# Convolution taps that read PSUM, and new step orders, in a twelve-stage fp32 block kernel on one Trainium2 core

## The reference, cut to what matters

```python
def causal_dwconv(x, w, b):            # CONV_W = 4 taps a channel
    y = lax.conv_general_dilated(x, w[:, None, :], window_strides=(1,),
        padding=((CONV_W - 1, 0),), dimension_numbers=("NWC", "WIO", "NWC"),
        feature_group_count=c)
    return y + b

def hybrid_mixer(h, w_in, w_out, ...):
    proj = h @ w_in
    pa, pb, pc = jnp.split(proj, [2 * A_WIDTH, 2 * A_WIDTH + B_IN], axis=-1)
    gate_a, rec_a = jnp.split(pa, 2, axis=-1)
    rec = causal_dwconv(rec_a, lru_conv_w, lru_conv_b)         # 384 channels
    ya = rg_lru(rec, ...) * jax.nn.gelu(gate_a)                # gated scan over time
    yb = ssd_mixer(pb, ...)      # silu(causal_dwconv(xbc)) on 896 channels, chunked state space
    yc = chunk_sgu(pc, ...)      # gelu, layer norm, masked 128 x 128 spatial mix
    return jnp.concatenate([ya, yb, yc], axis=-1) @ w_out
```

## Time and profile before

| | |
|---|---|
| median of 3 runs | 1957.23 us (1957.09 to 1957.32) |
| profiled execution | 1958.12 us |
| its span, first to last instruction | 1956.8 us |
| PE busy | 1926.5 us, 98% |
| DVE, ACT, POOL busy | 1204.0, 1098.7, 168.5 us (62, 56, 9%) |
| mean granted TensorE clock | 0.998 |
| DMA | 350 MB, 179 GB/s over the span |

### The profile page before, as it was taken

How to read it: one execution, slowest core, us unless ns; L and a number is a source line. 1 busy time by engine, 2 the same in 40 slices (tenths; PEclk the granted TensorE clock), 3 DMA queues, 4 the chain that set the end, 5 groups by cost and what they waited for, 6 DMA issues and landing times.

```text
span 1956.8 us, 24460 instructions
## 1 busy us (share of the span) xinstructions
PE 1926.5 (98%) x9304; PEld 1602.6 (82%) x9304; DVE 1204.0 (62%) x1863; ACT 1098.7 (56%) x1903; POOL 168.5 (9%) x219
## 2 busy tenths in 40 slices
PE   7999999999999999999999999999999999999999
PEld 6888888888788798888888888888888888888887
DVE  6555787555755578755665566665566556666554
ACT  5554776554655576655565555655555555565553
POOL 6000131000000013000000004100000000410000
PEclk9999999999999999999999999999999999999999
DMA  7564636554566463565465645355556554435553
GB/s 250 194 222 162 202 106 198 191 186 162 194 228 205 133 212 109 185 201 194 151 213 191 195 156 162 112 190 194 194 172 193 189 195 156 163 112 190 194 193 108
DMA packets 96773, 350.23 MB, mean 179 GB/s; under 512 B 10896, under 2 KB 11024, under 8 KB 96400
## 3 DMA queue, kind: packets, MB, share of 16 engines
q1 hardware_dynamic: 94176, 339.57, 52.2%
q10 hardware_dynamic: 2448, 9.09, 1.6%
q0 software_dynamic: 32, 0.00, 0.0%
HBM read 347.57 MB, written 1.05 MB: 178 GB/s over the span
## 4 chain that ended last, share of the span: by engine, by line
PE 90%; DVE 4%; POOL 2%; issue 1%; ACT 1%; DMA 0%; SPq 0%; ACTq 0%; POOLq 0%; DVEq 0%
PE ps_gu L397 18%; PE ps_gu L399 17%; PE ps_gu L398 17%; PE ps_acc L397 9%; PE ps_acc L399 9%; PE ps_acc L398 9%; PE ps_tr L444 2%; PE ps_gu L630 1%; PE ps_gu L631 1%; PE ps_gu L632 1%; DVE sb_wl L1867 1%; PE ps_acc L417 1%; DVE sb_scratch L2067 1%; DMA sb_x<-x 0%; DVE sb_wl L1862 0%
## 5 line engine op out<-in xcount | busy, mean ns | idle before, releaser
L397 PE MATMUL ps_gu<-sb_wh,sb_xh 128*128 128x512 f32 (+2 forms) x1600 | 642.8, 402 | 6.1 <-DVE sb_xl L1914 4.6
L399 PE MATMUL ps_gu<-sb_wh,sb_xl 128*128 128x512 f32 (+2 forms) x1600 | 624.3, 390 | 0.0
L398 PE MATMUL ps_gu<-sb_wl,sb_xh 128*128 128x512 f32 (+2 forms) x1600 | 621.9, 389 | 0.0
L1862 DVE SCALAR_TENSOR_TENSOR sb_wl<-sb_raw,sb_gpre,sb_wh 128x512 fp32r<-128x512 f32 x352 | 263.3, 748 | 244.5 <-ACT sb_wh L1190 244.5
L1867 DVE TENSOR_TENSOR sb_wl<-sb_raw,sb_wh 128x1024 fp32r<-128x1024 f32 (+2 forms) x296 | 359.5, 1232 | 47.2 <-ACT sb_wh L1193 46.2
L397 PEld LDWEIGHTS ps_gu<-sb_wh,sb_xh 128*128 128x128 f32 x1600 | 301.1, 188 | 65.4 <-DVE sb_xl L1914 6.9
L399 PEld LDWEIGHTS ps_gu<-sb_wh,sb_xl 128*128 128x128 f32 x1600 | 300.7, 188 | 63.3
L1193 ACT ACTIVATE sb_wh<-sb_raw 128x1024 fp32r<-128x1024 f32 (+2 forms) x296 | 306.0, 1045 | 77.8 <-DMA sb_raw<-stream 61.2
L398 PEld LDWEIGHTS ps_gu<-sb_wl,sb_xh 128*128 128x128 f32 x1600 | 301.8, 189 | 54.5
L1189 ACT ACTIVATE sb_wh<-sb_raw,sb_gpre 128x512 fp32r<-128x512 f32 x352 | 251.9, 716 | 138.9 <-PE ps_acc L399 134.7
L397 PE MATMUL ps_acc<-sb_wh,sb_fr 128*128 128x512 f32 (+1 forms) x768 | 301.0, 392 | 1.2 <-DVE sb_fr L1925 0.9
(11 more groups left out here) (258 smaller groups left out, 1541.2 us busy)
## 6 DMA issues: line engine op xcount, KB each, us to landing
sb_raw<-stream SPq DMA_DIRECT2D x628, 512.0 KB, 4.4
sb_raw<-stream SPq DMA_DIRECT2D x8, 416.0 KB, 3.3
sb_raw<-stream SPq DMA_DIRECT2D x8, 390.0 KB, 3.4
sb_gpost<-post_gains ACTq DMA_DIRECT2D x6, 512.0 KB, 6.7
sb_params<-params ACTq DMA_DIRECT2D x2, 1128.5 KB, 8.7
sb_scratch<-gain_rows ACTq DMA_DIRECT2D x4, 512.0 KB, 6.8
sb_raw<-stream SPq DMA_DIRECT2D x4, 384.0 KB, 3.4
sb_x<-x SPq DMA_DIRECT2D x2, 512.0 KB, 6.7
```

The lines of the kernel that those rows point to most:

```text
L397: pe.matmul(out, xh, wh, start=start, stop=False)
L398: pe.matmul(out, xh, wl, start=False, stop=False)
L399: return pe.matmul(out, xl, wh, start=False, stop=stop)
L1862: stt(m.wl[:, u % RING, 0:512], m.raw[:, u % RAW, 0:512], m.gpre[:, e, k:k + 1], m.wh[:, u % RING, 0:512].bitcast(F32), ALU.mult, ALU.subt ...
```

## The change

`conv_in`, its four slots and their zero columns are gone. `conv_first` keeps its one operation on ACT (tap of the newest column, bias). The three taps on DVE read the tile where PE left it, in the bank `m.gu[(n + 3) % 2]`, 253, 254 and 255 columns of it, and the first three, two, one columns of `conv` are left as they are. A bank is held until the last tap: `conv_tile(n)` from the third on waits for DVE's `conv(n - 2)`.

```diff
-        self.conv_in = m.then(CONV_SLOTS, 3 + T)
+        self.turns = m.then(2, 80)
...
         def conv_tile(n):
-            pe.wait_ge(*A.at(f"gate{n + 1}" if n < 2 else f"conv{n - 2}", l))
+            pe.wait_ge(*(A.at(f"gate{n + 1}", l) if n < 2 else V.at(f"conv{n - 2}", l)))
             tile(n + 3, m.gu[(n + 3) % 2][:, 0:T])
...
         def conv_first(n):
             act.wait_ge(*E.at(f"tile{n + 3}", l))
-            if n >= CONV_SLOTS:
-                act.wait_ge(*V.at(f"conv{n - CONV_SLOTS}", l))
-            src = m.gu[(n + 3) % 2][:, 0:T]
-            go(m1.conv_in[:, n % CONV_SLOTS, 3:3 + T], src, ACT.Copy)
...
         def softplus_exp():
-            act.wait_ge(*V.at("sp in", l))
+            for step in ("dt0", "dt1", "sp lambda"):
+                act.wait_ge(*V.at(step, l))
...
         def conv(n):
-            if n == 0:
-                vec.wait_ge(*G.at("pads", l))
             vec.wait_ge(*A.at(f"conv{n}", l))
             for i in range(3):
                 if i:
                     vec.wait_ge(*own(f"tap{n} {i - 1}", l))
-                v = stt(m1.conv[:, n, :], m1.conv_in[:, n % CONV_SLOTS, i:i + T],
-                        m.p1(taps)[:, i * c + j:i * c + j + 1], m1.conv[:, n, :], ALU.mult, ALU.add)
+                back = 3 - i
+                v = stt(m1.conv[:, n, back:T], m.gu[(n + 3) % 2][:, 0:T - back],
+                        m.p1(taps)[:, i * c + j:i * c + j + 1], m1.conv[:, n, back:T], ALU.mult, ALU.add)
```

```diff
     def post(f, e):
-        split(1)
+        hidden_low(f, LAST - 1, 1)
         split(1)
         hidden(f, LAST, 0)
-        hidden_low(f, LAST - 1, 1)
+        split(1)
         hidden_low(f, LAST, 0)
+        split(1)
+        split(1)
+        split(1)
+        post_mean(e, 0)
         post_scale(e, 0, 0)
-        post_mean(e, 0)
+        post_add(e, 0, 0)
```

More of the change, by code:

```diff
@@ L1748, in mix2 @@
         split(1)
-        latent_squares(1)
-        latent_high(0)
+        latent_high(1)
+        up_squares(0)
+        head_roots(0)
+        split(1)
+        value_out(0)
+        rotary_out(1, 0)
+        split(1)
+        split(1)
+        rotary_out(0, 1)
+        split(1)
+        value_out(1)
+        up_squares(1)
+        queries_out(0)
+        split(1)
+        head_roots(1)
+        split(1)
+        keys_out(0)
+        rotary_out(1, 1)
+        split(1)
+        split(1)
+        queries_out(1)
+        keys_out(1)
+        retention_values(0)
+        rotary_turned(0, 1)
+        split(1)
+        rotary_turned(0, 0)
+        split(1)
+        weights(1, 0)
+        retention_values(1)
+        split(1)
+        rotary_turned(1, 0)
+        rotary_turned(1, 1)
+        weights(0, 0)
+        split(1)
+        weights_out(0, 0)
+        weights(1, 1)
+        table(SILU)
+        split(1)
+        retained_squares(0)
+        weights_out(1, 0)
+        split(1)
+        silu_gate(0)
+        weights_out(1, 1)
+        attended_high(0)
         split(1)
@@ L2246, in mix1 @@
         split(1)
-        v_stats(0)
+        split(1)
+        decay_sums()
+        v_stats(1)
+        v_norm(1)
+        split(1)
+        split(1)
         conv(2)
-        decay_sums()
-        v_norm(1)
+        split(1)
         conv(1)
+        v_norm(0)
+        split(1)
         split(1)
@@ L2291, in mix1 @@
         split(1)
-        yn_low(1)
         post_scale(e + 1, 0, 0)
         post_mean(e + 1, 0)
+        yn_low(1)
         post_scale(e + 1, 0, 1)
         post_add(e + 1, 0, 0)
+        post_add(e + 1, 0, 1)
         split(1)
-        post_add(e + 1, 0, 1)
         x_low(e + 1, 0, 0)
         split(1)
+        split(1)
+        x_low(e + 1, 0, 1)
+        post_mean(e + 1, 1)
         post_scale(e + 1, 1, 0)
-        post_mean(e + 1, 1)
-        x_low(e + 1, 0, 1)
         post_scale(e + 1, 1, 1)
@@ L2306, in mix1 @@
         post_add(e + 1, 1, 1)
+        x_mean(e + 1, 0)
         split(1)
-        x_mean(e + 1, 0)
         x_low(e + 1, 1, 0)
         x_mean(e + 1, 1)
+        x_low(e + 1, 1, 1)
+        hidden(f + 1, 0, 0)
         split(1)
-        hidden(f + 1, 0, 0)
-        x_low(e + 1, 1, 1)
         split(1)
@@ L2473, in mix2 @@
         split(1)
+        hidden(f, LAST, 1)
         split(1)
-        hidden(f, LAST, 1)
         update(e, 0, 0)
@@ L2525, in mix2 @@
         masked(1, 0)
+        largest(1, 0)
         split(1)
-        largest(1, 0)
+        split(1)
         masked(0, 0)
```

505 lines of the change are left out of this document (222 added, 283 removed).

## The result

The changed kernel took 1940.76 us (median of 4 runs, 1940.6 to 1941.36) against 1957.16 before: ratio 0.9916, 95% interval 0.9903 to 0.9928. That is faster by 16.4 us, where 7.1 were forecast and the range ended at 1942.

What follows compares the result with a forecast made beforehand. The tensor engine was busy 1926.5 of 1956.8 us, so only its waits and lower-clock stretches could change. Terms -5.8 -1.9 -2.6 +2.4 +2.9 -2.1 = -7.1 took the median from 1957.23 to 1950.1 us; 8-in-10 range 1942 to 1958.

Steps and rivals of the forecast that it cites:

- The taps: Convolution taps on DVE reading PSUM: 480 against 485 ns, no difference taken; should stay near 0.5 us beside POOL.
- turn_inputs: In the mixer, after silu_x: stall 0.8 us instead of 2.2, no lower clock; 2.9 saved a mixer, -5.8 us.
- The waits of the second half: Behind turn_inputs in the mixer: POOL's decayed scores start earlier, so waits of 0.27 and 1.4 us go, -1.9 us.
- 0.55 throughout: Hand-over of the two PSUM banks between conv_tiles: 2.35 us against 2.9, slack 0.55 us, so nothing lost.
- Tail of this mixer: End of the mixer: yn_low(1) and yn_high(1) come later, turn_x(1,0) and gate_up(1,0) late; +2.4 us for two.
- post: Two `post` stretches: three gained splits before post_mean(0) on DVE, stalls 2.3 us against 0.85; +2.9 us for two.
- Boundary before this mixer: Before each mixer of that kind: reordered queues leave waits of 2.0 us against 3.3; -2.6 us for both.
- the mask's move: On POOL, the mask of w_s goes behind v_gain(0): its 1.3 us are covered by four conv_tiles (11.5 us).
- mix2: Two `mix2` stretches: of 3.0 us of waits each, 1.6 stay, the others go, two of 0.2 come; -2.1 us.
- C: Rival, chance 0.21: the new stalls in `post` and the mixer's tail are absent, 1945 us; with the boundary's gone, 1941.
- B: Rival, chance 0.07: slow taps from PSUM hold the bank, conv_tiles wait and silu_x is late; +9.1 us, 1966 us.
- A: Rival, chance 0.20: new waits at boundaries, `post` and tail eat the gain; about 1956 us.

Runs made afterwards that it cites:

- orders only: The changed kernel with its new orders, but the taps read an SBUF copy again (ACT copy, four slots and old wait of conv_tile back): 1950.7 us, ratio 0.997.

## Why the prediction was right in part and wrong in size

**Right.** The taps: 0.482 us at the median and 0.485 at most, none slow beside POOL, as the row of L1919 had it. The Trainium skill's 65 ns more for an operation from PSUM (VectorE: DVE Perf Modes, the section on the TRN2 errata) is not in these rows. Its GPSIMD Engine Reference ("Specifications") says that GpSimd shares its SBUF interfaces with VectorE and contends with operations that have two SBUF inputs; the runs here agree: 5.89 against 2.93 us for six taps, 2.41 against 1.42 for two normed.

turn_inputs: a stall of 0.8 forecast, 0.59 measured, and no lower clock: -3.1 a mixer for -2.9, in the profiled executions. Of this the sum counted the lower clock, 1.5, twice, as the profiled execution has it; by the mean clock of 0.999 the median had it about once. The waits of the second half went as forecast, and the second mixer gained 1.3 more than the first, as its 1.4 for L2713 suggests. No tile waits for a tap; between a last tap and the next tile in its bank are 0.1 to 0.7 us at four hand-overs and over 1.3 at the others, not 0.55 throughout.

**Wrong: the sum's two positive terms.** This is the step that failed: a lateness of DVE and ACT that the prediction carried on to later steps of PE, +5.3 us in the sum and about +0.6 measured. "Tail of this mixer", +2.4, was about 0.4: yn_low(1) made output(1,5) wait 0.20 (0.3 forecast), but the 7.5 us from there to post_mean(1) were 7.0, post_add(1,0) ended just before turn_x(1,0) was due, and the other stalls never came. In "post", +2.9, was +0.2. The first links of the chain were right: turn_x(0,1) lost 0.77 (0.95 forecast) and the next gate_up 0.41 (0.45), as DVE and PE show:

```profile
480.57 0.75 DVE L1859 SCALAR_TENSOR_TENSOR sb_wl<-sb_raw,sb_gpre,sb_wh 128x512 fp32r<-128x512 f32 x1 [0.34 <-ACT sb_wh L1190]
481.24 0.74 DVE L1861 SCALAR_TENSOR_TENSOR sb_wl<-sb_raw,sb_gpre,sb_wh 128x512 fp32r<-128x512 f32 x1
481.90 0.21 DVE L1878 TENSOR_SCALAR sb_stat<-sb_stat 128x1 f32<-128x1 f32 x1
```

```profile
485.07 0.65 PE L416 MATMUL ps_acc<-sb_const,sb_x 128*128 128x128 f32 x4 [0.61 <-DVE sb_x L1885]
486.11 0.47 PE L396 MATMUL ps_gu<-sb_wh,sb_xh 128*128 128x512 f32 x1 [0.17 <-issue]
```

but a stall of PE gives every later step the same time back, and I had carried the second half's lateness on as if PE had not already waited: of 0.2 and 0.6 came 0 and 0.28. Stalls over 0.13 start to start rose there only from 1.04 to 1.46.

**Wrong: two negative terms too small.** These two, -4.7 in the sum, were about -8.5. "Boundary before this mixer": 2.0 left of 3.3 forecast, 1.2 measured. I named the mask's move and gave it no price, only cover for its 1.3 us on POOL; undone alone it costs 1.0 a mixer, and the trace of before showed its effect on DVE, a normed of 1.76 us:

```profile
198.78 1.76 DVE L1908 SCALAR_TENSOR_TENSOR sb_scratch<-sb_x,sb_stat,sb_scratch 128x512 f32<-128x512 f32 x1
```

```profile
198.71 1.28 POOL L2671 TENSOR_TENSOR sb_params<-sb_params,sb_const 128x512 f32<-128x512 f32 x1
```

The 1.0 is more than the 0.8 a mixer by which the boundary's term was short. "mix2": the split's wait went, that for POOL's L2793 turned into one of 0.7 for L2378, and the boundary kept 1.2 of my 1.6, with a new 0.3 beside it; the segments gained 2.15 each against 1.05. In `mix1` the stalls and the slow clock account for about 5 of the first 6.0 (4.6 if only gaps over 0.13 us are counted, 5.4 by the terms above), in `mix2` for 1.1 to 1.3 of 2.15; the rest is in gaps under 0.13 us, and its cause stays open. So most of what `mix2` gave beyond the forecast came from nothing that the prediction had in its sum.

**The rivals.** It came out nearest to C, which I had at 0.21, with stalls "each taken at full length with hand-overs": `post` and the tail lost almost nothing. That the time agrees with its end, 1941, is luck: the end needed the boundary's stalls gone as well (4.0), of which 2.4 are still there, and the unexplained gains in `mix2` and in the small gaps made up for them. B's mechanism, tiles that wait for taps, is real, and in the old order costs 15.8 us with taps of 0.5 us; that the taps' place in DVE's list can bring it about, without a slow tap, I had not seen. A was the opposite of what happened.

## What to carry to other kernels

Where a PSUM bank is held for another engine's reads, that engine has to do them at once: move those reads ahead of the splits and scans in its list in the same edit, or the edit can be a loss (here +0.8%). Keep large GpSimd operations away from VectorE operations with two SBUF inputs that the tensor engine waits for, or give those an operand in PSUM. When stalls are walked through, count every later step anew from the end of each stall; each wait that PE takes pays for the next.

## What the runs showed that was not expected

A wait alone does not say whether the clock falls. In the kernel with only the new taps PE waited 2.51 us at a tile, longer than the 2.0 before turn_inputs that lost the clock, and kept 1.00, in both mixers; in the same run the 3.86 at 242.43 lost it. The row of the first and the windows at it, then at the second:

```profile
279.39 0.38 PE L630 MATMUL ps_gu<-sb_xh,sb_wh 128*128 128x256 f32 x1 [2.51 <-DVE sb_scratch L2063]
```

```profile
277.00:279.00 2.00, 0.00 (x0) 0.00 (x0) 1.89 (x5) 1.95 (x3) 0.96 (x1) 1.00 0.00 0
279.00:281.00 2.00, 1.61 (x13) 1.61 (x14) 1.78 (x4) 0.27 (x1) 0.86 (x1) 1.00 0.00 0
281.00:283.00 2.00, 2.00 (x19) 2.00 (x19) 0.75 (x2) 0.43 (x1) 1.08 (x1) 1.00 0.00 0
```

```profile
242.00:244.00 2.00, 1.57 (x7) 1.58 (x8) 1.97 (x4) 0.00 (x0) 0.00 (x0) 0.50 0.83 270
```

Not even the same wait in the same list decides it. With orders only, turn_inputs waits 3.4 us in each mixer, and the profiled execution lost the clock at the first and kept it at the second:

```profile
280.22 1.11 PE L638 MATMUL ps_gu<-sb_const,sb_scratch 128*128 128x128 f32 x4 [3.39 <-ACT sb_scratch L1479]
759.41 0.77 PE L638 MATMUL ps_gu<-sb_const,sb_scratch 128*128 128x128 f32 x5 [3.38 <-ACT sb_scratch L1479]
```

```profile
280.00:282.00 2.00, 1.78 (x8) 1.69 (x9) 0.85 (x2) 0.16 (x1) 0.00 (x0) 0.50 0.00 0
760.00:762.00 2.00, 2.00 (x14) 1.73 (x13) 2.00 (x4) 0.00 (x0) 0.91 (x1) 1.00 0.00 0
```

What differs between such places was not tried. It also limits the segment table: a stretch at the lower clock is worth some 1.5 us, and one profile shows one draw of it.

Outside the passages that were edited the trace repeats to 0.04 us in the steady stretches of 120 to 300 us between the mixers. The `mix2` segments do not: with no edit in them they came out up to 0.27 us shorter than in the changed kernel, and once 0.8 longer. So one profile tells a term of 0.2 us in the first kind of stretch, but not in a segment that holds a mixer.
